# A two-layer decoder trunk with top-2-of-8 experts: tokens of the later experts by way of a DRAM scratch and eight transposes

## The reference, cut to what matters

```python
def _swiglu(x, wg, wu, wd):
    return (jax.nn.silu(x @ wg) * (x @ wu)) @ wd

def _moe(x, router, wg, wu, wd):
    logits = (x @ router).astype(jnp.float32)
    top_val, top_idx = lax.top_k(logits, TOP_K)
    top_w = jax.nn.softmax(top_val, axis=-1)
    gate = jnp.sum(jax.nn.one_hot(top_idx, N_EXPERTS, dtype=jnp.float32) * top_w[..., None], axis=-2)
    y = jnp.zeros_like(x)
    for e in range(N_EXPERTS):
        y = y + gate[..., e:e + 1].astype(x.dtype) * _swiglu(x, wg[e], wu[e], wd[e])
    return y

def reference(...):
    ...
    h = h + _even_mixer(_rmsnorm(h, norm_mix_even[i]), ...)
    h = h + _swiglu(_rmsnorm(h, norm_ffn_even[i]), ffn_wg[i], ffn_wu[i], ffn_wd[i])
    ...
    h = h + _odd_mixer(_rmsnorm(h, norm_mix_odd[i]), ...)
    h = h + _moe(_rmsnorm(h, norm_ffn_odd[i]), router[i], moe_wg[i], moe_wu[i], moe_wd[i])
    return _rmsnorm(h, final_norm)
```

## Time and profile before

| | before |
|---|---|
| median of 3 runs | 1461.03 us |
| profiled execution | 1464.81 us |
| its span, first to last instruction | 1463.0 us |
| mean granted clock of TensorE | 0.988 of 2.4 GHz |
| PE busy | 1414.0 us, 97% |
| DVE busy | 1162.0 us, 79% |
| ACT busy | 1016.0 us, 69% |
| POOL (GpSimd) busy | 17.5 us, 1% |
| moved by DMA | 418.96 MB, mean 286 GB/s |

### The profile page before, as it was taken

One profiled execution on the slowest core, in us unless ns is written; L12 is line 12 of the kernel. 1 busy time (PEld: TensorE's weight loads), 2 busy tenths in 40 slices (PEclk: granted clock), 3 DMA queues, 4 the chain that ended last, 5 costly groups with the idle time before them and its releaser, 6 DMA issues.

```text
span 1463.0 us, 20271 instructions
## 1 busy us (share of the span) xinstructions
PE 1414.0 (97%) x7069; PEld 1180.0 (81%) x7070; DVE 1162.0 (79%) x1225; ACT 1016.0 (69%) x1183; POOL 17.5 (1%) x25
## 2 busy tenths in 40 slices
PE   8989999999899999999999999999999999999995
PEld 6778989987778887888888788888878888887884
DVE  4665655556469998998998999899899989989994
ACT  5654544466348777777877877787787778778773
POOL 1200000000000000000000000000000000000000
PEclk9999999999999999999999999999999999999998
DMA  9365454344468998998999899799989989989930
GB/s 334 136 209 180 173 192 154 130 155 169 172 246 322 369 369 297 370 368 317 347 364 372 297 373 368 292 375 371 338 324 373 368 292 375 371 320 343 372 132 29
DMA packets 175888, 418.96 MB, mean 286 GB/s; under 512 B 3702, under 2 KB 7964, under 8 KB 175852
## 3 DMA queue, kind: packets, MB, share of 16 engines
q1 hardware_dynamic: 174800, 415.40, 77.7%
q0 software_dynamic: 976, 3.05, 0.7%
q10 hardware_dynamic: 76, 0.02, 0.0%
HBM read 417.41 MB, written 1.05 MB: 286 GB/s over the span
## 4 chain that ended last, share of the span: by engine, by line
PE 90%; DVE 4%; ACT 3%; issue 1%; DVEq 1%; DMA 0%; ACTq 0%
PE ps L1359 25%; PE ps L1361 25%; PE ps L1360 24%; PE ps L1579 3%; PE ps L1581 3%; PE ps L1580 3%; PE ps L1823 2%; PE ps L1854 2%; ACT w_hi L470 1%; DVE w_lo L822 1%; DVE w_lo L1259 1%; DVE h L1334 1%; PE ps L1892 1%; PE ps L1893 1%; PE ps L1381 0%
## 5 line engine op out<-in xcount | busy, mean ns | idle before, releaser
L1259 DVE TENSOR_TENSOR w_lo<-ring_a,w_hi 128x1024 fp32r<-128x1024 f32 x384 | 456.9, 1223 | 38.4 <-ACT w_hi L734 35.0
L734 ACT ACTIVATE w_hi<-ring_a 128x1024 fp32r<-128x1024 f32 x384 | 399.7, 1059 | 74.5 <-PE ps L1361 73.8
L1259 DVE TENSOR_TENSOR w_lo<-ring_b,w_hi 128x1024 fp32r<-128x1024 f32 x288 | 345.3, 1224 | 33.5 <-ACT w_hi L734 29.0
L1359 PE MATMUL ps<-w_hi,xg_hi 128*128 128x512 f32 x896 | 358.6, 400 | 10.6 <-DVE w_lo L1259 8.8
L1361 PE MATMUL ps<-w_hi,xg_lo 128*128 128x512 f32 x896 | 353.4, 394 | 0.0
L1360 PE MATMUL ps<-w_lo,xg_hi 128*128 128x512 f32 x896 | 351.8, 393 | 0.0
L734 ACT ACTIVATE w_hi<-ring_b 128x1024 fp32r<-128x1024 f32 x288 | 301.4, 1058 | 58.1 <-PE ps L1361 58.1
L822 DVE TENSOR_TENSOR w_lo<-ring_a,w_hi 128x1024 fp32r<-128x1024 f32 (+2 forms) x119 | 141.9, 1199 | 125.8 <-ACT w_hi L470 125.7
L470 ACT ACTIVATE w_hi<-ring_a 128x1024 fp32r<-128x1024 f32 (+2 forms) x119 | 122.2, 1033 | 136.2 <-PE ps L1361 70.0
L1359 PEld LDWEIGHTS ps<-w_hi,xg_hi 128*128 128x128 f32 x896 | 168.4, 188 | 51.1 <-DVE w_lo L1259 13.3
L1361 PEld LDWEIGHTS ps<-w_hi,xg_lo 128*128 128x128 f32 x896 | 168.6, 188 | 39.7
(11 more groups left out here) (296 smaller groups left out, 1455.7 us busy)
## 6 DMA issues: line engine op xcount, KB each, us to landing
ring_a<-in_moe_wg SPq DMA_DIRECT2D x40, 2048.0 KB, 7.9
ring_a<-in_moe_wu SPq DMA_DIRECT2D x32, 2048.0 KB, 8.3
ring_b<-in_moe_wd SPq DMA_DIRECT2D x32, 2048.0 KB, 7.7
ring_b<-in_moe_wu SPq DMA_DIRECT2D x24, 2048.0 KB, 8.5
ring_a<-in_moe_wd SPq DMA_DIRECT2D x24, 2048.0 KB, 7.8
ring_b<-in_moe_wg SPq DMA_DIRECT2D x16, 2048.0 KB, 7.6
ring_a<-in_ffn_wg SPq DMA_DIRECT2D x5, 2048.0 KB, 8.9
ring_a<-in_ffn_wu SPq DMA_DIRECT2D x5, 2048.0 KB, 7.8
```

Of the source, the lines that this page charges most:

```text
L734: nc.scalar.activation(w_hi[:, (Q1 + q) % NQ, 0:1024], slot(j % RING2)[:, 1024 * k:1024 * k + 1024], ACT.Copy).then_inc(hi_done, 1)
L1259: v.tensor_tensor(w_lo[:, (Q1 + q) % NQ, 0:1024], slot(j % RING2)[:, 1024 * k:1024 * k + 1024], w_hi[:, (Q1 + q) % NQ, 0:1024].bitcast(F32 ...
L1359: pe.matmul(out_, a_hi, w_hi[:, q, c0:c1], start=first, stop=False)
```

## The change

Each later expert's tokens are not gathered by a product with `pick`. The normed tokens stay float32 in a buffer of their own (`tokens`; no halves are made of them). DVE works out for each token its two rows in a DRAM scratch `xs` of 12 x 128 rows (`token_rows`, 12 short instructions after `extras`, ahead of the loop). GpSimd (POOL) clears `xs` with one broadcast DMA during the dense stage, and after `rows_done` scatters the tokens with four indirect DMAs. SP loads the 128 rows of item n (0.5 MB) into `xg_rows` between units 10 and 11 of the item before. `gather(n)` for n over 0 is then 8 transposes. `gather(0)` still multiplies with `pick`, as 16 products in float32 in place of 32 in float32r. In both cases PSUM holds the float32 columns in banks 0 and 1, ACT rounds them to `xg_hi`, and DVE's `xg_lo` is now PSUM minus `xg_hi` and so waits for ACT (`xg_head`).

At the start the gains of the first norm have a semaphore of their own (`lead_gain_in`) and are turned first; then come 8 products of filler in place of 11; the other gains are turned after the first quantum of q. ACT makes one copy as soon as the identity is in, ahead of its wait for the gains. Four and three products of filler stand between the groups of transposes. The numbering `fills` loses its first entry. In the routing `keep_pace(10)` is `keep_pace(5)`, and `keep_pace(4)` stands behind `gather(0)`.

```diff
@@ sync @@
+            def load_tokens(n):
+                sp.wait_ge(xs_in, 16 * 2 * T)
+                sp.wait_ge(gathered, n)
+                sp.dma_start(xg_rows[:, :], xs[n]).then_inc(xg_loaded, 16)
             for j in range(RING2, UI):
                 load(j, 0, 0)
+                if j == 10:
+                    load_tokens(1)
...
+                    if j == 10:
+                        load_tokens(i + 1)
@@ gpsimd @@
             pool.wait_ge(h_done, 2)
+            pool.memset(zeros[:, :], 0.0).then_inc(zeroed, 1)
...
+            pool.wait_ge(zeroed, 1)
+            pool.dma_start(xs.rearrange("n p d -> p n d"), zeros[:, :].rearrange("p (u d) -> p u d", u=1).to_broadcast(
+                [P, ITEMS + 1, D])).then_inc(xs_cleared, 16)
             pool.wait_ge(xn_done, T)
             gains((A["final_norm"], D))
+            pool.wait_ge(xs_cleared, 16)
+            pool.wait_ge(rows_done, 1)
+            for t in range(T):
+                for n in range(2):
+                    pool.indirect_dma_start(xs.rearrange("n p d -> (n p) d"),
+                                            bass.IndirectOffsetOnAxis(row_of[:, t, n:n + 1], 0), tokens[:, t, :],
+                                            None).then_inc(xs_in, 16)
@@ scalar @@
-            act.wait_ge(gcol_done, 1)
+            act.wait_ge(ident_in, 16)
+            copy(st("TABLE"), ident[:, 0:1], ACT.Copy)
+            act.wait_ge(lead_gain_done, 1)
...
+            act.wait_ge(xs_cleared, 16)
             qk_even("qk_d", 4, kT2, D_QK)
...
-            for t in range(T):
-                act.wait_ge(xn_done, t + 1)
-                copy(xn_hi[:, t, :], xn[:, t, :], ACT.Copy).then_inc(xn_head, 1)
             act.wait_ge(top_done, 1)
@@ vector @@
+            lo_upto(5)
+            dve.wait_ge(gains_turned, 1)
+            link(v.tensor_copy(gcol[:, KC:NG], ps[:, 4, KC:NG]))
...
             def gathered_rests(n):
-                dve.wait_ge(gathered, n + 1)
-                v.tensor_copy(xg_lo[:, :, :], ps[:, 2:4, :].rearrange("p b (c s) -> p (b c) s", s=P)).then_inc(xg_rest, 1)
+                dve.wait_ge(xg_head, n + 1)
+                v.tensor_tensor(xg_lo[:, :, :], ps[:, 0:2, :].rearrange("p b (c s) -> p (b c) s", s=P),
+                                xg_hi[:, :, :].bitcast(F32), ALU.subtract).then_inc(xg_rest, 1)
             choose(0)
-            for t in range(T):
-                dve.wait_ge(xn_head, t + 1)
-                v.tensor_tensor(xn_lo[:, t, :], xn[:, t, :], xn_hi[:, t, :].bitcast(F32), ALU.subtract).then_inc(xn_rest, 1)
...
             for q in range(NQ, AHEAD):
                 expert_rest(0, q)
+            token_rows()
             v.memset(st("LEFT"), 0.0).then_inc(added, 1)
@@ tensor @@
-            for _ in range(11):
-                pe.matmul(ps[:, 5, 0:P], ident, ident, start=True, stop=True)
-            pe.wait_ge(grow_in, 16 * 7)
-            pe.transpose(ps[:, 6 + k % 2, 0:NG], grow[0:NG, :], ident[0:NG, 0:NG]).then_inc(t_ready[k % 2], 1)
+            pe.wait_ge(lead_gain_in, 16)
+            pe.transpose(ps[:, 5, 0:KC], grow[0:KC, :], ident[0:KC, 0:KC]).then_inc(lead_gain_turned, 1)
+            keep_pace(8, 3, P)
             pe.wait_ge(x_in, 16 * T)
             for f in range(4):
                 turn("mix_even", f, h_chunk)
+                if f == 1:
+                    keep_pace(4, 3, P)
+                elif f == 2:
+                    keep_pace(3, 3, P)
...
-            keep_pace(10)
-            pe.wait_ge(xn_rest, 2)
-            def gather(n):
+            keep_pace(5, 5, 256)
+            pe.wait_ge(xn_done, 2)
+            def gather(n, moved):
                 pe.wait_ge(picked, n + 1)
-                for part, x in enumerate((xn_hi, xn_lo)):
-                    for c in range(KC):
-                        o = ps[:, 2 * part + c // 4, P * (c % 4):P * (c % 4 + 1)]
+                if moved:
+                    pe.wait_ge(xg_loaded, 16 * n)
+                for c in range(KC):
+                    o = ps[:, c // 4, P * (c % 4):P * (c % 4 + 1)]
+                    if moved:
+                        ins = pe.transpose(o, xg_rows[:, P * c:P * (c + 1)], ident)
+                    else:
                         for t in range(T):
-                            ins = pe.matmul(o, x[:, t, P * c:P * (c + 1)], pick[:, t, :], start=(t == 0), stop=(t == T - 1))
+                            ins = pe.matmul(o, tokens[:, t, P * c:P * (c + 1)], pick[:, t, :], start=(t == 0),
+                                            stop=(t == T - 1))
...
-            gather(0)
+            gather(0, False)
+            keep_pace(4, 5, 256)
...
-                    gather(i + 1)
+                    gather(i + 1, True)
                     down(FB - 1)
```

More of the change, by code:

```diff
@@ L161, in trunk @@
     fills, n = {}, 0
[L162 removed]
+    for name, k in (("mix_even", 4), ("sgu_w", 1), ("qk_a", 8), ("mixed", 2), ("p0_a", 1), ("ob", 2),
                     ("p1_a", 2), ("oa", 2), ("ffn", 4), ("rrow", 1), ("mix_odd", 4), ("cq", 2), ("ckv", 1), ("qk_d", 8),
@@ L200, in trunk @@
         xn = sbuf("xn", [T, D])
-        xt_hi = sbuf("xt_hi", [KC, S], F32R)
-        xt_lo = sbuf("xt_lo", [KC, S], F32R)
+        turned = ExitStack()
+        xt_hi = sbuf("xt_hi", [KC, S], F32R, on=turned)
+        xt_lo = sbuf("xt_lo", [KC, S], F32R, on=turned)
+        turned.close()
+        tokens = sbuf("tokens", [T, D])
+        xg_rows = sbuf("xg_rows", [D])
+        sbuf("spare", [D])
         gain = sbuf("gain", [D])
@@ L228, in trunk @@
         rrow = sbuf("rrow", [S], on=dense)
+        zeros = sbuf("zeros", [D], on=dense)
         dense.close()
@@ L255, in trunk @@
         wts = sbuf("wts", [T, 4], on=route)
+        rows = sbuf("rows", [T, ITEMS], on=route)
+        valid = sbuf("valid", [T, ITEMS], on=route)
         route.close()
@@ L263, in trunk @@
         y_lo = sbuf("y_lo", [D], F32R)
-        pick = sbuf("pick", [T, SLOTS], F32R)
+        pick = sbuf("pick", [T, SLOTS])
         pickT = sbuf("pickT", [S], F32R)
@@ L320, in trunk @@
         rwg_done = sem("rwg_done")
-        xn_done, xn_head, xn_rest = sem("xn_done"), sem("xn_head"), sem("xn_rest")
+        xn_done = sem("xn_done")
+        zeroed, xs_cleared, rows_done, xs_in, xg_loaded = map(sem, (
+            "zeroed", "xs_cleared", "rows_done", "xs_in", "xg_loaded"))
         picked, gathered, pickT_ready, pickT_done, xg_head, xg_rest = map(sem, (
@@ L1370, in turn, with keep_pace @@
                 ins.then_inc(t_ready[k % 2], 1)
+            def keep_pace(n, bank, w):
+                for _ in range(n):
+                    pe.matmul(ps[:, bank, 0:w], ident, table[:, 0:w], start=True, stop=True)
             def h_chunk(c, t):
@@ L1450, in _ @@
                 projection(q, kq, 512, (0, 1)).then_inc(q_used, 1)
+                if kq == 0:
+                    pe.wait_ge(grow_in, 16 * 6)
+                    pe.transpose(ps[:, 4, 0:NG], grow[0:NG, :], ident[0:NG, 0:NG]).then_inc(gains_turned, 1)
             for kq in range(4):
@@ L1775, in _ @@
                             turn("router", f, h_chunk)
-            def keep_pace(n):
-                for _ in range(n):
-                    pe.matmul(ps[:, 5, 0:256], ident, table[:, 0:256], start=True, stop=True)
             def logits(c0, c1):
```

62 lines of the change are left out of this document (43 added, 19 removed).

## The result

| | before | after |
|---|---|---|
| median | 1460.97 us (4 runs) | 1445.12 us (4 runs) |
| lowest and highest | 1460.05 to 1461.89 us | 1442.22 to 1446.88 us |
| profiled execution | 1464.81 us | 1442.22 us |
| its span | 1463.0 us | 1440.5 us |
| mean granted clock in it | 0.988 | 0.995 |

The ratio is 0.9881, 95% interval 0.9867 to 0.9895: the change makes the kernel 1.2% faster, 15.9 us between the medians. The forecast was 1440.3 us with a range of 1436.5 to 1446.5. Between the two profiled executions the gain is 22.6 us, between the medians it is 15.9 us, and the sum of the prediction had been 20.7 us. Three numbers for one change: what lies between them is the subject of most of what follows.

A forecast was written before the change was run, and what follows sets the result against it. PE, busy 125.74 of 126.80 us per item, was taken as the bound. Items 16.3, start 3.7 and routing 0.7 make 20.7 us off 1464.81, 1444.1; less 3.8 us gives 1440.3 us, range 1436.5 to 1446.5.

The forecast's parts named there:

- The end of an item: Last down block of each item: eight transposes replace 32 matmuls, PE starts 2.04 us earlier, then limited by `hT_lo`.
- of 16.3 us for eight: Expert items: the 2.04 us saved at each item's end, carried over to eight items as 16.3 us.
- What lies behind it: After `hT_lo`: later `xg_lo` covered by 3.7 us, DVE's low half by 1.0 us; the 1.1 us wait stays.
- The start: Kernel start: 2.2 us from earlier turning and table load, 1.6 us from the clock, less 0.1; sum 3.7 us.
- The bound that I named: Start: the second weight unit's first low half, there at 23.2, limits the gain to not over 4.7 us.
- The routing: Routing: item 0 starts 1.6 us earlier, against a slow stretch and `token_rows`; net 0.7 us gained.
- The loads, the clearing and the scatters: DMA: 0.5 MB more per item, 6.3 MB of scratch clearing and four scatters, costed at zero.
- The third rival: Item 0: SP stands at the scatters past 483, each us costing one; 1472 us at 515; chance 0.05.
- the first rival: Items: the clock falls once per item, 1.6 us each, 12.8 us for eight, giving 1453.1 us; chance 0.06.
- The last step of the sum: Total: the median's 3.8 us below the profiled execution carried over, from 1444.1 to 1440.3 us.
- the second rival: Transposes at float32 pace, or start and routing give nothing: 1445.0 or 1444.7 us; chance 0.12.
- The low end's own terms: Range's low end, 1436.5: start at 4.7, routing at 1.6, one slow clock stretch fewer elsewhere.

The follow-up runs named there:

- realigned: Changed kernel with the dummy products of fill_all and 8 words less in the unused pad (70 to 62): 1438.35 us median, ratio 0.9838.
- fill_all: Changed kernel with dummy products in four idle places of TensorE (even attention's output, odd mixer, odd attention's output, item 0): 1440.81 us median, ratio 0.9857.
- double_turns: Changed kernel with each of the eight transposes of a later gather made twice, same result: 1444.39 us median, ratio 0.9880.
- after_again: The changed kernel unaltered, timed again: 1442.55 us median, 1441.69 to 1445.63 us, ratio 0.9865.
- before_shift: Kernel before the change with 8 words more in the unused pad (78 to 86): 1465.57 us median, lowest 1462.64 us, ratio 1.0021.

## Why the prediction was right and where it was wrong

**The end of an item: the step was right, its carry to the whole item was not.** Eight transposes in 0.91 us (0.94 predicted), the down block 0.13 us behind `hT_lo` (0.1 predicted), `hT_lo` next in the waits. With 8 words less in the pad (realigned) the period is 124.52 us, 2.05 us less than 126.57, where 2.04 had been worked out. The kernel as changed gets 1.67 us; of the other 0.38 us, 0.34 are taken by the placement of the buffers (124.86 us in fill_all against 124.52 in realigned). The failing step is "of 16.3 us for eight": it priced the instructions of the diff and passed over its declarations. Eight times a little over 0.3 us is the 2.5 us that realigned won.

**What lies behind it: right.** `xg_lo` and `w_lo` show in no new wait, the low half that PE waits for is still 1.1 us per item (7.2 us in 7, against 7.4 of the earlier trace rows), `y_lo` holds PE once, 1.4 us, in the last item only. The doubled transposes add that PE has 0.6 us to spare in front of `hT_lo`.

**The start: right, 4.1 us for 3.7.** The first product of q comes at 12.1 (12.6 predicted) where it came at 14.91, q is read out at 23.91 (24 for the next projection's begin), and the clock stays at 1.00 where it had been 0.50. So 2.8 us come ahead of that product (2.2 taken) and 1.3 us behind it (1.5 taken). The bound that I named was not reached: ACT waits 2.13 us at 20.38 for the second unit to land, but its first low half is there at 22.70 and PE begins k at 23.7, and the view of PE's waits lists none from its first product of q to 60 us.

**The routing: every step seen, the net at its low end.** Item 0 starts 1.8 us earlier against the last addition into `h` (20.38 us before, 18.61 after; 1.6 predicted). The slow stretch behind it came, from 425.1, and cost 1.5 us; up to 1.6 had been named as the bound, and my net of 0.7 us took half of it. `token_rows` costs nothing: in realigned the stretch from the second quantum to the last hidden group is 110.71 us, as in the kernel before (110.72), so its 0 to 0.5 us is 0. The second quantum follows the first 5.34 us later and no longer 5.64. So 1.8 + 0.3 - 1.5 - 0.3 for the placement is the 0.3 us of the table.

**The loads, the clearing and the scatters: right at nothing.** Taking the loads of rows away changed no item, and the clearing costs no more than 0.1 us, as worked out with fill_all. SP's queue in the timeline of after:

```profile
444.82 0.43 SPq L407 DMA_DIRECT2D xg_rows<-xs  x1
450.01 0.37 SPq L393 DMA_DIRECT2D ring_b<-in_moe_wg  x1
```

The load of rows, which needs the four scatters, is issued at 444.82, 0.5 us behind unit 10, so SP does not stand at them, and unit 11 is issued at 450.01, where it was 459.20. The third rival counted from 483 and is out.

**The clock at the ends of items.** PEclk is 1.00 in all items of after, though the end of an item is transposes and a short idle time, and the item window of double_turns, with sixteen in a row, reads 1.00 too. That it could fall there, the first rival, was a guess of mine that no row showed. Neither the odd mixer nor these ends show a fall behind transposes, and that rival is out. What part transposes have in the falls stays open all the same: between two products PE had nothing but transposes and idle time for 1.9 us at an item's end, 2.2 us in double_turns and 2.7 us in the odd mixer, but for 3.0 to 3.7 us ahead of the three slow stretches of before, where it had turned eight, too.

**The last step of the sum was wrong: 3.8 us carried over.** I took the profiled execution's 1464.81 us, subtracted 20.7, and then took off 3.8 us more because the median lay that much lower. That difference is no cost of profiling which a changed kernel would have as well. It is the granted clock: the profiled execution of before was one of those with three more slow stretches (0.988 against 0.992), and in the four sets of the experiments 21 of its 58 runs took 1463 us or more. (No execution of before on its lower level was profiled. An estimate from the profile fits, though: three stretches of 3.4 us at half the clock take 0.0035 off the mean of a span of 1463 us.) The same stretches could be absent from the profile of the changed kernel, as they were in the 1442.22 us one. Had I subtracted 20.7 us from the lower level, 1460.2, the forecast would have been 1439.5; the changed kernel at that level takes 1442.0. The 2.5 us between them are the placement, since the start's 0.4 us more and the routing's 0.4 us less cancel; the rest of the way to the median, 1445.12, is runs that fell on the upper level.

So the range held in part by luck. Its high end was worked out from the second rival, dearer transposes or nothing from start and routing, which did not come, and from one slow stretch more. What lifted the median instead was a placement that no term held, and slow stretches ahead of the routing in half of the runs (the profile of after_again, at 1445.63 us, has two). (The low end's own terms give 1436.8 and not 1436.5.)

## What to carry to other kernels

Before a gain is set against a time, put the runs in order by granted clock and compare level with level; a fill of idle places that costs little can bring all runs to the faster level, here 4.7 us of spread down to 0.3. Read the declarations of a diff like its instructions: where the buffers behind them land can be part of the change, here 8 words of a pad for 2.5 us, and a stretch in which both kernels issue the same work is the place where it shows. When work is taken from an engine, look for the operand that comes next, since all that is saved beyond it is idle time.

## What the hardware showed that was not expected

Eight words more in the unused pad ahead of the items' operands lengthen the mean step of the float32r products of 128x512, from 0.2312 us in realigned to 0.2317 us in fill_all and from 0.2312 us in before to 0.2316 us in before_shift. That is 0.3 us in 96.4 us, in every item, at a granted clock of 1.00. It is not spread evenly: the 32nd step between operand loads behind an item's first hidden group is 0.225 us in before and in realigned, and 0.236 or 0.237 us in before_shift, fill_all and after, while the step ahead of it goes from 0.234 to 0.231 or 0.232 us.

A slow stretch of the clock (0.50 for 3.4 us, at the start for 6.8 us) came behind places where PE had waited (busy 1.36 of 3.30 us in the row above), and it came in some executions and not in others: the three ahead of the routing together cost 4.6 us in the profiles of the changed kernel (382.0 against 377.4 us), and most runs of the unchanged kernel before lie near 1460.2 or 1464.3 us accordingly. Behind 22 transposes in a row, 2.2 us in double_turns, it did not come.
